# First 128 tokens of the memory layer by gathered table rows; dense products over 384 columns; low weight parts on VectorE after the choice

## The reference

```
s1, i1 = lax.top_k(s[:, :, 0], PEER_TOPK); s2, i2 = lax.top_k(s[:, :, 1], PEER_TOPK)
best, pos = lax.top_k(cand, PEER_TOPK)          # 16 x 16 candidates per head
eidx = i1 * PEER_N_KEYS + i2 (at pos);  gate = softmax(best)
act = gelu(einsum('td,thkd->thk', xb, u_tab[ib]), approximate=False) * gb
out = einsum('thk,thkd->td', act, v_tab[ib])
```

## Time and profile before

| | |
|---|---|
| median of three runs | 3349.07 us |
| profiled execution | 3348.17 us |
| its span | 3346.4 us |
| choice, gates, output stage | from 1768, 2135 and 2612 us |
| TensorE busy | 3061.1 us (91%) |
| VectorE, ScalarE, GpSimd busy | 1714.5, 1120.0, 1225.2 us |
| moved by DMA | 545.76 MB |

### The profile page before, as it was taken

One profiled execution on the slowest core, in us unless ns is written; L12 is line 12 of the kernel. 1 busy time (PEld: TensorE's weight loads), 2 busy tenths in 40 slices (PEclk: granted clock), 3 DMA queues, 4 the chain that ended last, 5 costly groups with the idle time before them and its releaser, 6 DMA issues. The chain is left out here.

```text
span 3346.4 us, 38769 instructions
## 1 busy us (share of the span) xinstructions
PE 3061.1 (91%) x14760; PEld 2391.8 (71%) x14764; DVE 1714.5 (51%) x2464; ACT 1120.0 (33%) x1697; POOL 1225.2 (37%) x388
## 2 busy tenths in 40 slices
PE   5887886989799999998799999899999899999996
PEld 2674774333488777787588888788888788888885
DVE  3946533111306283594408787668667344444445
ACT  2113532223323311573332333345444222222222
POOL 2220112222134432212233444567666344444442
PEclk8895778999799999899899999999999999999998
DMA  6720034999324442004213334253454655555551
GB/s 236 294 107 13 1 126 183 416 407 388 132 102 158 151 164 113 13 1 151 90 63 127 140 143 151 106 204 148 160 212 161 246 190 187 200 194 185 198 197 67
DMA packets 148698, 545.76 MB, mean 163 GB/s; under 512 B 17888, under 2 KB 84448, under 8 KB 106080
## 3 DMA queue, kind: packets, MB, share of 16 engines
q1 hardware_dynamic: 136480, 517.69, 41.8%
q0 software_dynamic: 11520, 24.15, 1.9%
q10 hardware_dynamic: 576, 2.27, 0.2%
HBM read 503.15 MB, written 92.27 MB: 178 GB/s over the span
## 5 line engine op out<-in xcount | busy, mean ns | idle before, releaser
L2411 POOL TENSOR_TENSOR w_lo<-ring,w_hi 128x2048 fp32r<-128x2048 f32 x127 | 617.4, 4861 | 701.0 <-ACT w_hi L2403 701.0
L178 PE MATMUL psum<-h_hi,w_hi 128*128 128x512 f32 x1808 | 727.2, 402 | 40.4 <-PEq L366 18.8
L180 PE MATMUL psum<-h_hi,w_lo 128*128 128x512 f32 x1808 | 713.9, 395 | 0.0
L179 PE MATMUL psum<-h_lo,w_hi 128*128 128x512 f32 x1808 | 713.6, 395 | 0.0
L159 POOL TENSOR_TENSOR w_lo<-ring,w_hi 128x2048 fp32r<-128x2048 f32 x64 | 304.0, 4750 | 737.6 <-ACT w_hi L152 697.3
L178 PEld LDWEIGHTS psum<-h_hi,w_hi 128*128 128x128 f32 x1808 | 345.8, 191 | 116.2 <-issue 46.5
L178 PE MATMUL psum<-a_hi,w_hi 128*128 128x512 f32 x1024 | 399.7, 390 | 11.7 <-issue 11.7
L179 PE MATMUL psum<-a_lo,w_hi 128*128 128x512 f32 x1024 | 399.4, 390 | 0.0
L180 PE MATMUL psum<-a_hi,w_lo 128*128 128x512 f32 x1024 | 399.3, 390 | 0.0
L180 PEld LDWEIGHTS psum<-h_hi,w_lo 128*128 128x128 f32 x1808 | 344.6, 191 | 74.9
L179 PEld LDWEIGHTS psum<-h_lo,w_hi 128*128 128x128 f32 x1808 | 345.8, 191 | 72.1 <-issue 1.7
(11 more groups left out here) (438 smaller groups left out, 4181.3 us busy)
## 6 DMA issues: line engine op xcount, KB each, us to landing
ring<-in_weights SPq DMA_DIRECT2D x199, 1024.0 KB, 4.9
w_expert_in<-in_experts_in SPq DMA_DIRECT2D x32, 2048.0 KB, 12.3
hid_dram<-hid_acts SPq DMA_DIRECT2D x64, 512.0 KB, 2.7
gates_dram<-block_gates SPq DMA_DIRECT2D x8, 4096.0 KB, 15.9
gate_tiles<-gates_dram SPq DMA_DIRECT2D x64, 512.0 KB, 6.8
hid_tiles<-hid_dram SPq DMA_DIRECT2D x64, 512.0 KB, 5.6
o<-in_ada_later SPq DMA_DIRECT2D x16, 1024.0 KB, 5.6
w_expert_down<-in_experts_down SPq DMA_DIRECT2D x16, 1024.0 KB, 13.2
```

The lines of the kernel that those rows point to most:

```text
L178: k.nc.tensor.matmul(out, hi, x_hi, start=start, stop=False)
L179: k.nc.tensor.matmul(out, hi, x_lo, start=False, stop=False)
L180: return k.nc.tensor.matmul(out, lo, x_hi, start=False, stop=stop)
L2411: k.nc.gpsimd.tensor_tensor(lo, slot(k, n), hi.bitcast(F32), ALU.subtract).then_inc(k.w_ready, 1)
```

## The change

The dense work leaves out tokens 0 to 127 (`DENSE` = 384 columns). Those 128 tokens are computed directly: for each of the 128 pairs, one indirect DMA of GpSimd gathers one table row of 1024 floats for each token (128 partitions, 512 KB): 128 gathers of `u` and 128 of `v`. VectorE multiplies a gathered `u` tile by the tokens and sums along the row (`row_dot`), and adds a gathered `v` tile times its weight into a running sum (`row_add`). The sum is transposed by TensorE into the open PSUM banks at the end. Other parts:

* The tokens for the dots are turned by TensorE (16 small products) into PSUM at the start of the choice stage and copied to `row_work`.
* 40 batches instead of 32 run in the choice stage, 8, 12, 12 and 8 around the four exponentials; 24 in the gates stage. 36 of the dots stand in the choice stage, between the pieces of VectorE's blocks 1 to 3 (`between`), their gathers behind GpSimd's weight splits 13 to 38; the other 92 dots stand in the gates stage.
* In the choice stage up to seven row buffers are in use; in the gates stage three; in the output stage seven.
* In the gates and output stages `split_low` is VectorE's. The second one-hot table is made with its gate at once, by 8 instructions of 128x128 with two operands per partition, instead of one of 128x1024 and a GpSimd multiplication. GpSimd issues only gathers there.
* ScalarE's `split_high` stands ahead of the second gelu of a batch.

```diff
+DENSE = SEQ - P
+CHOICE_LOOPS = (0, 2, 5, 8, 10)
+ROW_SLOTS, MORE_SLOTS = 3, 7
+EARLY_DOTS = 36
...
+def row_slots():
+    uses, last, plan = [0] * MORE_SLOTS, [-1] * MORE_SLOTS, []
+    for j in range(2 * PAIRS):
+        s = j % MORE_SLOTS if j < EARLY_DOTS else j % ROW_SLOTS if j < PAIRS else (j - PAIRS + ROW_SLOTS) % MORE_SLOTS
...
+def gather_row(k, pool, j):
+    s, _, last = ROW_PLAN[j]
+    pool.wait_ge(*k.row_read.at(last + 2))
+    pick = j % PAIRS
+    pool.indirect_dma_start(row_buffer(k, j), None, k.d["peer_u" if j < PAIRS else "peer_v"],
+                            bass.IndirectOffsetOnAxis(ap=k.row_index[:, pick:pick + 1], axis=0),
+                            bounds_check=PEER_KEYS * PEER_KEYS - 1, oob_is_err=False).then_inc(k.again_rows[s].sem, 16)
+def row_dot(k, dve, j, x_rows):
+    row = row_of(k, dve, j).rearrange("p (c n) -> p c n", n=x_rows.shape[-1])
+    k.nc.vector.scalar_tensor_tensor(row, row, 1.0, x_rows, ALU.mult, ALU.mult, accum_out=k.row_hid[:, j:j + 1]).then_inc(k.row_read.sem, 1)
+def row_add(k, dve, p):
...
+        ins = k.nc.vector.scalar_tensor_tensor(k.row_sum, row, k.row_hid[:, p:p + 1], k.row_sum, ALU.mult, ALU.add)
...
             mm = split_products(k, k.psum[:, 2 * parity + jj], w_hi[:, at:at + P], w_lo[:, at:at + P],
-                                k.h_hi[:, kc], k.h_lo[:, kc], kc == 0, kc == KC - 1)
+                                k.h_hi[:, kc, P:], k.h_lo[:, kc, P:], kc == 0, kc == KC - 1)
...  (choice stage, GpSimd and VectorE)
+                gathered = 0
+                first = early_batches // TT + 1
+                for b in range(early_batches):
+                    split_low(k, pool, b + 2)
+                    due = MORE_SLOTS + (b - first) * (EARLY_DOTS - MORE_SLOTS) // (early_batches - 4 - first) if b >= first else 0
+                    while gathered < min(due, EARLY_DOTS):
+                        gather_row(k, pool, gathered)
+                        gathered += 1
...
+                def between(t):
+                    nonlocal calls, dots
+                    if t >= 1:
+                        calls += 1
+                        while dots < min(EARLY_DOTS, (calls - 4) * EARLY_DOTS // 52):
+                            row_dot(k, dve, dots, x_rows)
+                            dots += 1
...  (gates and output stage, VectorE)
+    dots_behind = (3, 3, 3, 3, 3, 4, 6, 6)
+            for g in range(rounds):
+                for r in range(body):
+                    for blk, part, at in steps_behind(r) + (steps_within(r + 1) if r + 1 < body else []):
+                        hot_rows(2 * steps * g + at)
+                    for j in range(dots, min(dots + dots_behind[r], PAIRS)):
+                        row_dot(k, dve, j, k.x_rows)
+                        dots += 1
+                    split_low(k, nc.vector, body * (g0 + g) + r + 2)
...
+            def step(b):
+                adds = range(adds_due(b - 1) if b else 0, adds_due(b))
+                for p in adds[:1]:
+                    row_add(k, dve, p)
+                if b + 1 < BATCHES:
+                    low(b + 1, b + 1)
+                for p in adds[1:]:
+                    row_add(k, dve, p)
+                if 2 <= b + 1 < BATCHES:
+                    split_low(k, nc.vector, BATCHES + b + 1)
+                if b + 2 < BATCHES:
+                    multiply(b + 2, b + 2)
```

More of the change, by code:

```diff
@@ L2497, in _ @@
             def _(pool):
[L2498 to L2501, removed]
+                split_low(k, pool, 1)
+                gathered = 0
[6 more added lines that the diff above has]
+                        gathered += 1
             @block.vector
@@ L2505, in _, with best_of @@
                 step = k.vstep
-                def best_of(rows, values, places):
+                x_rows = k.psum[:, 6:8].rearrange("p b n -> p (b n)").unsqueeze(1)
+                calls, dots = 0, 0
+                def between(t):
[5 more added lines that the diff above has]
+                            dots += 1
+                def best_of(t, rows, values, places):
                     for r in range(0, K, 8):
+                        between(t)
                         for j, row in enumerate(rows):
@@ L2743, in low, with hot_rows @@
                                         ALU.subtract).then_inc(a_ready, 1)
-            def step(b, r):
-                if r + 1 < BATCHES:
-                    multiply(b + 1, r + 1)
-                    dve.wait_ge(batch_summed, b + 1)
-                    low(b + 1, r + 1)
+            def hot_rows(n):
+                b, first = n % 2, n * GROUP
+                dve.wait_ge(used, n + 1)
+                nc.vector.tensor_tensor(hot1[:, b], index1[:, first:first + GROUP].unsqueeze(2).broadcast_to(shape),
+                                        iota[:].unsqueeze(1).broadcast_to(shape), ALU.is_equal)
+                for i in range(GROUP):
+                    ins = nc.vector.tensor_scalar(hot2[:, b, i], iota[:], index2[:, first + i:first + i + 1], gate[:, first + i:first + i + 1],
+                                                  ALU.is_equal, ALU.mult)
+                ins.then_inc(hot, 1)
@@ L2751, in _ @@
             dve.wait_ge(loaded, earlier_loads + 16)
+            wait_parts(k, dve, body * g0 + 1)
             dve.sem_inc(used, 2)
-            with dve.Fori(0, SEQ // (2 * GROUP)) as g:
-                for b in range(2):
-                    n = 2 * g + b
-                    dve.wait_ge(used, n + 1)
-                    row = iota[:].unsqueeze(1).broadcast_to(shape)
-                    nc.vector.tensor_tensor(hot2[:, b], tokens(index2, n), row, ALU.is_equal).then_inc(hot, 1)
-                    nc.vector.tensor_tensor(hot1[:, b], tokens(index1, n), row, ALU.is_equal).then_inc(hot, 1)
+            dots = EARLY_DOTS
@@ L2760, in _ @@
             dve.sem_inc(batch_summed, 1)
             multiply(0, 0)
+            multiply(1, 1)
             low(0, 0)
-            each_step(dve, step)
+            dve.wait_ge(row_gelu, 1)
+            k.vstep(nc.vector.tensor_tensor(k.row_hid[:], k.row_hid[:], k.row_gate[:], ALU.mult))
+            for b in range(BATCHES):
+                step(b)
             for m in range(1, KC, 2):
@@ L2769, in _ @@
         def _(pool):
-            with pool.Fori(g0, g0 + rounds) as g:
-                for r in range(body):
-                    for blk, step, at in steps_behind(r) + (steps_within(r + 1) if r + 1 < body else []):
-                        n, b = 2 * steps * g + (at - 2 * steps * g0), step % 2
-                        pool.wait_ge(hot, 2 * n + 1)
-                        nc.gpsimd.tensor_tensor(hot2[:, b], hot2[:, b], tokens(gate, n), ALU.mult).then_inc(weighted, 1)
-                    split_low(k, pool, body * g + (r + 2), r + 2)
-            def split(b, r):
-                if r + 2 < BATCHES:
-                    split_low(k, pool, b + (BATCHES + 2), r + (BATCHES + 2))
-            each_step(pool, split)
+            for j in range(EARLY_DOTS, 2 * PAIRS):
+                if j == PAIRS:
+                    for i in range(2):
+                        pool.wait_ge(stored[i], 16 + 16 * rounds)
+                gather_row(k, pool, j)
         @block.tensor
```

142 lines of the change are left out of this document (98 added, 44 removed).

## The result

The changed kernel takes 3607.47 us (median of four runs, 3605.45 to 3615.88) against 3347.22 for the kernel before: a ratio of 1.0779, 95% interval 1.0756 to 1.0802. The prediction was wrong, in sign too: it said 3095. The profiled execution has a span of 3604.8 us.

The account below looks back on a forecast made before the run. TensorE, busy without a gap, was taken as the bound; 92 us less up to the first output product and 163 less in output made 3346.4 into 3091, taken as 3095, range 3000 to 3210.

Parts of the forecast that it names:

- Dense products: TensorE's 384-column matmuls in all three stages: 0.1725 us each, 8.28 us a batch, 2.60 less than before.
- Output stage: TensorE the bound at 530 us, VectorE 7.0 of 8.28 us a batch, 4 us charged for DMA; 536 us in all.
- The DMA sum: Output stage: weights, hidden values, gates and rows moved in 8.28 us a batch, 348 GB/s.
- Gates stage: VectorE the bound in batches 0 to 4, gathered rows with three buffers in 5 to 7; three rounds 363 us.
- the time from dot to landed row: Gates stage: 6 us from a dot until the next row has landed in its buffer.
- Choice: TensorE waits 37 us for weight splits behind gathers, low clock 4 us; stage 386 us instead of 367.
- The fourth: Rival, slower than before: gathers through full queues at 22.2 us, gates stage 751 us, whole 3480; chance 0.03.
- The second: Rival: gathers with three buffers bound the gates stage, 9 to 12 us dot to row, 3140 to 3195; chance 0.15.
- The first: Rival: TensorE stays the bound, rows land in 4.5 us, gates stage 294 + 15, whole about 3005; chance 0.15.
- the fifth: Rival, no change: 384 columns cost what 512 do in output and earlier stages, whole 3340; chance 0.01.
- The third: Rival: VectorE holds gathers, landing 2.5 us late, 35 us more in the gates stage, whole 3130; chance 0.12.
- the signs that the prediction named for being wrong: 384-column matmuls not starting 0.172 us apart, landings over 8 us, or an output stage that waits for anything.

Follow-up runs that it names:

- the first experiment: Changed kernel with SyncE's weight load in the output stage issued two batches later, behind the loads of hidden values and gates: 3199.14 us, ratio 0.9558 to the kernel before.
- experiment 4: Changed kernel without the 92 gathers issued in the gates stage, VectorE's dots running on stale rows: 3505.95 us.
- experiment 12: The first experiment with the choice's 36 dot products reading the tokens from SBUF instead of PSUM: 3200.85 us, ratio 0.9560 to the kernel before.

## Why the prediction was wrong, point by point

- **Dense products, right.** A batch takes 8.32 us where nothing waits (60 batches in the 500 us window of the first experiment), 8.28 predicted; all 64 batches of that stage, start and end with them, are 8.45 each.
- **Output stage, the step that failed.** "Weights and inputs are ready 2.7 us before TensorE asks": it compared amounts of work and DMA rates and put at nothing the order of SyncE's queue, past which the split had been moved. The two lines that mattered stood in the code, and the kernel before already showed VectorE waiting 4.7 us a batch for loads asked for behind a split. 7.0 us of VectorE (measured 6.4) were no bound, but 8.6 us of issue and landing lay behind them in a closed loop. The stage took 414 us more than forecast, where the prediction had charged 4 us for all of DMA; the first experiment gives 409 of them back. The DMA sum itself held: 348 GB/s computed, 336 measured there, with TensorE never idle.
- **Gates stage, mechanism right, size off.** A step at 3.2 us, a dot at 1.14 from start to start, a split at 2.28: batches of 15.2 (15.75 predicted). VectorE's own sum of 330 us stands (experiment 4: 335). The mis-sized term is the time from dot to landed row, 6 us: it was 9.4 in the median and 18 to 22 behind a store, and 4 MB stores were counted only in a mean rate over the round. Batch 3 of the second round took 23.4 us instead of 15.75, and batches 5 to 7 of the same round 59 instead of 43; three such rounds are 71 of the 78 us.
- **Choice, right but for the clock.** TensorE's waits for splits that stood behind gathers: 39.0 for 37, the three largest 12.3, 7.2 and 4.1 for 12, 10 and 5. The clock after them: 16 us instead of 4.
- **Rivals.** The fourth had the sign and named a place, but not this one: gathers at 22 us in the gates stage; the stage lost 78 us, not 390. The second (9 to 12 us from dot to row) is what the gates stage did: a median of 9.4, and +78 in its band of +45 to +100. The first fails by the gates stage's 447 us, the fifth by the 8.32 us a batch. The third, VectorE holding the gathers, is seen, and is small: mean issue 1.49 us over 91 gathers where 0.99 is the least, so half a microsecond late in the mean, not 2.5. In the gates stage 21 issues beside a split took 2.3 or 3.05 us:

```profile
2340.16 2.29 DVE L2421 TENSOR_TENSOR w_lo<-ring,w_hi 128x2048 fp32r<-128x2048 f32 x1
...
2340.26 3.05 POOL L2450 DMA_INDIRECT rows<-in_peer_u,row_index  x1 [0.30 <-DVE rows L2465]
```

It ends 0.86 us after the split does, and so do, within 0.01 us, all 78 issues of the gates and output stages that began beside one, so that the issue is held until the split is done. The Trainium skill, on the page SBUF — State Buffer, in the section on SBUF's two sides, has two such holds. One is narrower than the prediction's sentence on it: in its two-port modes VectorE keeps GpSimd from writing the descriptors of its DMAs. By the other, a VectorE instruction with two inputs in SBUF shuts out a GpSimd instruction that reads SBUF. The split has two inputs in SBUF, and the issue takes its row numbers from `row_index` in SBUF, so the second fits this trace by its sign; which of GpSimd's accesses is held, no run here shows.
- **Range and chances.** 3000 to 3210 left out all cases in which two engines wait for each other through a third one's queue. Of the 0.04 for slower, 0.03 stood for gathers through full queues, which is not what happened. With that one loop opened the kernel takes 3199, inside the range, but 104 us above the forecast: the gates stage's 78 and the choice's 21 stay. Two of the signs that the prediction named for being wrong came true, landings over 8 us (up to 19.9 from the issue) and an output stage that waits.

## What to carry to other kernels

When work moves from one engine to another, look at who waits for its result, and in the DMA-issuing engine's program at every transfer behind that wait: if the mover's next instruction needs one of these, a landing time is added to each turn of the loop, and no rate or busy share shows it. Put transfers that wait for little ahead of those that wait for much. A gather whose buffer comes free late should be priced beside the largest store that can be in flight, and each idle time of TensorE with the products at the lower clock behind it (here 1.5 to 3 us for each idle time of 2.7 us and more).

## What the runs showed of the hardware

- Behind idle times of 2.7 to 12.3 us TensorE started its next 9 to 19 products of 384 columns 0.32 us apart (1.2 GHz) and the rest 0.173 apart. A longer idle time had no longer slow stretch behind it: 9 products behind 12.3 us, 13 behind 2.7. Over the choice this cost 16 us beside 39 us of waits.
- An indirect DMA's issue on GpSimd takes 0.99 us alone. If it begins while VectorE's weight split runs (both inputs in SBUF), it ends 0.86 us after the split, up to 3.06 us long in the gates stage. In the choice none of the 38 issues took over 1.04 us, 11 of them beside dots with one operand in PSUM; with that operand in SBUF (experiment 12) three took 1.7 to 1.8.
- The output stage's traffic, which ran at 184 GB/s when each load was asked for late, ran at 336 GB/s in the first experiment, with the DMA engines busy 0.94 and TensorE busy in all of the window's 500 us.
